# Sample attention of a hybrid decoder layer: the order of the second sequence's key pages and the first sequence's decay rows on SyncE's queue

## The reference

```
def forget_attention(q, k, v, dq, dk, q_pos, k_pos):
    s = jnp.einsum('bqhd,bkhd->bhqk', q, k).astype(jnp.float32) * (HEAD_DIM ** -0.5)
    s = s + jnp.transpose(dq, (0, 2, 1))[..., None] - jnp.transpose(dk, (0, 2, 1))[:, :, None, :]
    mask = k_pos[None, :] <= q_pos[:, None]
    s = jnp.where(mask, s, -jnp.inf)
    p = jax.nn.softmax(s, axis=-1)
    return jnp.einsum('bhqk,bkhd->bqhd', p.astype(v.dtype), v)
...
    k_past = cache_k[l][page_table].reshape(Bs, -1, ATT_HEADS, HEAD_DIM)
    v_past = cache_v[l][page_table].reshape(Bs, -1, ATT_HEADS, HEAD_DIM)
    lf_past = cache_logf[l][page_table].reshape(Bs, -1, ATT_HEADS)
```

## Time and profile before

| | us |
|---|---|
| median of the three runs | 2130.13 |
| lowest and highest run | 2128.33, 2132.96 |
| the profiled execution, its own time | 2126.76 |
| its span, first to last instruction | 2124.7 |
| TensorE matmul busy | 2014.1 (95% of the span) |
| VectorE, ScalarE, GpSimd busy | 795.1, 390.1, 628.2 |
| mean granted TensorE clock | 0.987 of full speed |

### The profile page before, as it was taken

One profiled execution on the slowest core, in us unless ns is written; L12 is line 12 of the kernel. 1 busy time (PEld: TensorE's weight loads), 2 busy tenths in 40 slices (PEclk: granted clock), 3 DMA queues, 4 the chain that ended last, 5 costly groups with the idle time before them and its releaser, 6 DMA issues.

```text
span 2124.7 us, 33015 instructions
## 1 busy us (share of the span) xinstructions
PE 2014.1 (95%) x13046; PEld 1916.5 (90%) x13046; DVE 795.1 (37%) x1429; ACT 390.1 (18%) x699; POOL 628.2 (30%) x487
## 2 busy tenths in 40 slices
PE   5989988799999999999999998999999999999996
PEld 4978887545899999999999997999999999999996
DVE  3445556534100233012621766143224422441337
ACT  3434445422100000000211244000000000000003
POOL 4321111023522232233232533432323222232322
PEclk9999999999999999999999999999999999999999
DMA  9322112387423112241111501111111111111112
GB/s 332 101 66 62 38 34 81 100 265 256 144 79 89 41 43 87 70 129 45 43 50 40 164 1 31 50 46 43 40 49 39 49 39 49 39 43 46 40 40 85
DMA packets 174969, 164.17 MB, mean 77 GB/s; under 512 B 14255, under 2 KB 138627, under 8 KB 174748
## 3 DMA queue, kind: packets, MB, share of 16 engines
q1 hardware_dynamic: 153451, 132.50, 20.3%
q0 software_dynamic: 6400, 17.05, 2.5%
q10 hardware_dynamic: 15032, 13.43, 2.0%
HBM read 149.03 MB, written 14.03 MB: 77 GB/s over the span
## 4 chain that ended last, share of the span: by engine, by line
PE 85%; DVE 5%; SPq 4%; issue 2%; ACT 2%; POOL 1%; DMA 1%; ACTq 0%; POOLq 0%; DVEq 0%
PE psA L1777 11%; PE psA L1781 11%; PE psA L1783 11%; PE psB L1777 10%; PE psB L1781 10%; PE psB L1783 10%; PE psB L1891 2%; PE psB L1895 1%; PE psB L1894 1%; PE psA L1945 1%; PE psB L2055 1%; PE psA L2030 1%; PE ps L1959 1%; DVE prob L1284 1%; SPq L410 1%
## 5 line engine op out<-in xcount | busy, mean ns | idle before, releaser
L644 POOL CAST whi<-raw 128x1024 fp32r<-128x1024 f32 x131 | 136.7, 1043 | 1135.8 <-PE psA L1777 544.1
L645 POOL TENSOR_TENSOR wlo<-raw,whi 128x1024 fp32r<-128x1024 f32 x131 | 320.8, 2449 | 10.5
L1777 PE MATMUL psA<-hhi,whi 128*128 128x364 f32 (+1 forms) x1008 | 222.6, 329 | 3.0 <-DVE stat L1368 1.6
L1781 PE MATMUL psA<-hlo,whi 128*128 128x364 f32 (+1 forms) x1008 | 222.0, 328 | 0.0
L1783 PE MATMUL psA<-hhi,wlo 128*128 128x364 f32 (+1 forms) x1008 | 221.6, 328 | 0.0
L1777 PE MATMUL psB<-hhi,whi 128*128 128x364 f32 (+1 forms) x960 | 211.3, 328 | 0.6 <-DVE alo L1393 0.6
L1781 PE MATMUL psB<-hlo,whi 128*128 128x364 f32 (+1 forms) x960 | 211.5, 328 | 0.0
L1783 PE MATMUL psB<-hhi,wlo 128*128 128x364 f32 (+1 forms) x960 | 211.1, 328 | 0.0
L1647 DVE TENSOR_TENSOR ft<-psB,sil 128x1092 f32<-128x1092 f32 x22 | 28.5, 1296 | 405.1 <-PE psB L1783 398.3
L1777 PEld LDWEIGHTS psA<-hhi,whi 128*128 128x128 f32 x1008 | 173.3, 188 | 3.8 <-issue 3.4
L1783 PEld LDWEIGHTS psA<-hhi,wlo 128*128 128x128 f32 x1008 | 174.9, 188 | 0.0
(11 more groups left out here) (421 smaller groups left out, 3619.9 us busy)
## 6 DMA issues: line engine op xcount, KB each, us to landing
raw<-in_w_in SPq DMA_DIRECT2D x53, 512.0 KB, 3.9
raw<-in_w_gate_up SPq DMA_DIRECT2D x44, 512.0 KB, 3.8
kpage<-in_cache_k SPq DMA_DIRECT2D x64, 256.0 KB, 4.1
vpage<-in_cache_v POOLq DMA_DIRECT2D x64, 256.0 KB, 4.0
ada_late<-in_ada_w SPq DMA_DIRECT2D x8, 2048.0 KB, 8.0
raw<-in_w_down SPq DMA_DIRECT2D x22, 512.0 KB, 3.7
ada<-in_ada_w SPq DMA_DIRECT2D x4, 2048.0 KB, 17.5
x_keep<-xt SPq DMA_DIRECT2D x1, 4368.0 KB, 21.6
```

What stands on the lines that cost most here:

```text
L644: link(nc.gpsimd.tensor_copy(whi[slot][:, 0:n, :], raw[slot][:, 0:n, :]))
L645: nc.gpsimd.tensor_tensor(wlo[slot][:, 0:n, :], raw[slot][:, 0:n, :], whi[slot][:, 0:n, :].bitcast(F32), ALU.subtract).then_inc(s["w_split ...
L1777: m = mm(ps[:, c, 0:CW[c]], whi[slot][:, b, :], hi[:, k, chunk(c)], start=first, stop=False)
L1781: mm(ps[:, c, 0:CW[c]], whi[slot][:, b, :], lo[:, k, chunk(c)], start=False, stop=False)
```

## The change

Ahead of the loop, the first two pairs of sequence 1's key pages are issued before the decay rows of sequence 0 and not behind them. No transfer is added or taken away, no wait is added, and the loop behind is untouched. The other engines' instructions stay as they were (their line numbers are two higher).

```diff
@@ -509,9 +509,11 @@
-            decay_loads(0)
-            for q in range(4):
-                key_loads(1, q)
+            key_loads(1, 0)
+            key_loads(1, 1)
+            decay_loads(0)
+            key_loads(1, 2)
+            key_loads(1, 3)
             with sp.Fori(1, DB - 1) as b:
```

## The result

The changed kernel takes 2132.88 us (median of 22 runs, 2127.27 to 2138.11); the kernel before, run 22 times beside it, 2129.97 us (2124.43 to 2133.95). The ratio is 1.0017, with a 95% interval of 1.0010 to 1.0024: slower by about 3.6 us, or 2.9 us by the medians. The forecast was 2130.8 us, within 0.2%, in a range of 2127.6 to 2134.0.

What follows compares the result with a forecast made beforehand. TensorE bounds the kernel, its first sample pass lengthened 3.66 us by late key pages. The larger of pair 2's +0.7 and the decay rows' +0.5 us, added to 2130.13, gave 2130.8 us; range 2127.6 to 2134.0.

Steps and rivals of the forecast that it cites:

- decay rows' cover of 3.7 us: First pass, VectorE: time from the decay rows' landing at 412.73 to L1363 at 416.47, forecast to be used up.
- pair 2 would slip: SyncE's queue, first pass: sequence 1's third pair of key pages issued 0.7 us later, landing at 422.7.
- the forecast's own bounds: Whole kernel: -0.7 to +1.6 us, so 2129.4 to 2131.7 us, given a chance of 0.75.
- every later pass would be shifted by the same amount: Passes behind the first: the 0.7 us lost at L2040 carried in full to the end.
- decay rows move back: SyncE's queue, first pass: issue ends 5.7 us later, VectorE waits, L2040 starts at 423.6, +0.5 us.
- the +0.7 of the sum: L2040, first pass: maximum of the pair 2 path, +0.7 us, and the decay row path, +0.5 us.
- the landing of the decay rows: First pass: taken at 419.7, 6.0 us from the issue of the last, with bounds 417.4 and 420.6.
- the stretch of 422.3 to 424.7: First pass: the times between which L2040 should start in the changed profile.
- C: First pass: decay rows land much later, each microsecond past 419.2 costing one; at 423.5, 2134.4 us; chance 0.03.
- B: L2055, first pass: TensorE's low clock covers its matmuls, 2134.5 us if all, 2132.6 if half; chance 0.14 together.
- A: First pass: the whole 3.66 us of extra time goes, giving 2126.5 us; chance 0.08.
- D: First pass: landings only swap and L2040 stays at 423.1, giving 2130.1 us; chance counted within the forecast's 0.75.

Runs made afterwards that it cites:

- run 22: Not a label but a count: the kernel before, unedited, was run 22 times beside the changed kernel; median 2129.97 us.
- e8: Changed kernel with GpSimd holding all of sequence 0's value pages until the decay rows had landed; first pass 25.95 us.
- e2: Kernel before, with all four pairs of sequence 1's key pages issued ahead of the decay rows; first pass 25.63 us against 19.38.
- e7: Kernel before, with pairs 0, 1 and 2 of sequence 1's key pages issued ahead of the decay rows; first pass 24.92 us against 19.38.
- e10: Kernel before, with sequence 1's page numbers read ahead into registers and the value pages' second half held until the decay rows landed; 2127.19 us, ratio 0.9988.

## Why the prediction was right, and where it was not

**Right**: that TensorE's waits for key pages in the first pass would go and give nothing; that the decay rows' cover of 3.7 us would be used up and VectorE's wait for them become the real one; the times of issue (first key page at 409.99, on before's clock 407.95 against 407.8; decay rows from 411.7 to 414.4 against 411.6 to 414.3); that pair 2 would slip (its first page went out at 418.16, on before's clock 0.5 us later than forecast, and by the time it landed nothing waited for it); that the sixteen matmuls of L2055 would keep their full speed.

That the time lies in the range is luck in part. 2132.88 us is above the forecast's own bounds, 2129.4 to 2131.7. The range reached to 2134.0 because of the spread of the runs and of the rival with the low clock, and neither is what happened. (Its upper end adds 2.3 us of spread where the runs of before show 2.8, and no reason is given.)

**Wrong**: that every later pass would be shifted by the same amount. The fourth pass of the kernel before has a wait of 0.60 us for value pages that nearly goes in the changed kernel, so 0.5 us of the first pass's loss comes back (0.9 in the second pair of traces). The prediction had read the rows of one later pass, the third, and took them for all.

**Wrong in size**: the term "decay rows move back", +0.5 us at L2040, and with it the +0.7 of the sum. The first pass lost 3.31 us (3.2 in the second pair of traces). The step that failed is the landing of the decay rows, taken at 5.4 us behind the end of their issue with 6.3 as the upper bound, from the flight of a key page issued at the same time. They took 7.7 and 7.5. VectorE's wait for them was 10.06 us, where 5 to 8 had been expected. L1363 was to start at 420.05 and started at 424.63, on before's clock 422.6, and L2040 at 426.3, outside the stretch of 422.3 to 424.7 that was named as the test. A later pass's 3.1 us and the first pass's 4.1 were taken as the near rows of the other end; both stand in emptier stretches (in the later pass the transfer engines' share was 0.56 in 460 to 464 us, and in the first pass the rows went out while it was 0.00 to 0.45, against 0.93 to 0.98 in the changed kernel). The rows' size (0.27 MB) was given as a reason to go below the flight of a page. It was none: with only their own queue's bytes about (e8) they took 1.9 us.

**The rivals.** C, the late decay rows, is the mechanism that came true, though less far than it was set: its rule, one microsecond for each past 419.2, gives 422.14 - 419.2 = 2.9 us of the 3.3; the rest is 0.1 us between mask and maximum and 0.2 us in the transposes behind, where the granted clock was half (424 to 430 us). It was given a chance of 0.03 because its time was set at a 4.3 us loss; the ground between 1.6 and 4.3 us had no case that covered it by this cause. B, the low clock over L2055, did not happen there: the sixteen matmuls took 3.65 us (3.84 in the second trace). It was a fair rival, since the longer waits of e2 and e7 brought part of it. A, the full gain, did not happen, and D, no change, neither. The sentence from the Trainium skill's "DMA: Bandwidth & Descriptors" (section "Latency and other measured facts") puts most of a fixed cost of about 2 us at the access to HBM under high load. The 1.9 us of e8 are near it. The changed kernel is not: by that sentence the rows would have landed near 417, and on before's clock they landed at 422.1. The prediction did not follow it, and the measurement bears that out.

**What the argument missed** is the same in both directions: the prediction gave each queue its own clock (issue time plus a flight) and took the flight from a row. Flights here are the result of all the bytes that cross, so moving one transfer changes its flight too. In the kernel before, SyncE's decay rows went out at 405.9 to 408.6, when no key page could be issued yet (`kt_tr` stood below 2 until 407.02) and the transfer engines were idle, as two windows of the kernel before show (the last two numbers are the transfer engines' share and GB/s):

```profile
405.00:407.00 2.00, 1.36 (x11) 0.95 (x9) 0.95 (x4) 1.10 (x4) 0.37 (x1) 1.00 0.00 0
407.00:409.00 2.00, 1.38 (x12) 1.12 (x12) 1.19 (x2) 0.80 (x2) 1.09 (x2) 1.00 0.45 122
```

That hole was the cheapest place for them. The change leaves it empty and puts the rows into a full stretch. Of the changed kernel, whose stage starts at 407.97:

```profile
408.00:410.00 2.00, 1.67 (x13) 1.40 (x14) 1.60 (x5) 0.74 (x2) 0.90 (x2) 1.00 0.00 0
```

## What to carry to other kernels

When several queues feed the same transfer engines, ask which stretch is empty and which is full before moving a transfer; a transfer that gives way to another lands later by the other queue's backlog too, not only by its own delay of issue. Look for a wait's second place before shortening it: here the keys, the decay rows and the values were each within a few microseconds of being the last, and the only edit that shortened the pass clearly (e10) had all three nearly in time. When a trace offers flights from 3 to 7 us for the same kind of transfer, the bound of a moved one should go past the longest of them.

## What the runs showed of the hardware that was not expected

The delay of the same four transfers on the same queue behind the same four pages was 1.9, 4.2 or 7.7 us, by what another engine's queue had issued (none, four or eight value pages of 256 KB). The same rows issued first on their queue took between at most 3.4 and 5.4 us, and that spread is not explained.

TensorE's clock differs between executions of one kernel. Behind the last scores TensorE does the same work in all traces and is busy for 3.6 to 5 of every 5 us. There the first trace of the kernel before shows full clock, and its second a stretch at a lower grant, as the changed kernel does. Of the first trace of the kernel before, around the same gap in the work:

```profile
550.00:555.00 5.00, 3.63 (x22) 3.16 (x22) 0.88 (x2) 2.55 (x3) 0.95 (x1) 1.00 0.22 40
```

of the changed kernel's first trace:

```profile
555.00:560.00 5.00, 3.62 (x15) 3.21 (x15) 0.88 (x2) 2.33 (x3) 0.85 (x1) 0.66 0.15 29
560.00:565.00 5.00, 5.00 (x23) 5.00 (x22) 0.00 (x0) 0.21 (x1) 0.00 (x0) 0.66 1.03 382
```

and of the second trace of the kernel before:

```profile
555.00:560.00 5.00, 4.41 (x19) 4.39 (x19) 0.19 (x1) 2.55 (x3) 0.00 (x0) 0.66 0.63 197
```

It costs 2.9 us in the changed kernel's first trace (the fifth line of the table of stretches), and appeared in 13 of the 14 traces, in all kinds of kernels, by more or less. In the prompt's attention too the mean grant in 340 to 407 us was 0.92 in one trace and 0.82 in the other of each kernel, and the one of 0.82 belongs to before once and to after once. Why an execution gets the one or the other was not tried. So single profiled executions of this kernel can't be compared by their spans: the stretch that holds the edit has to be.
